# Two programs merged into one at the front of a two-layer kernel: projection 1 and attention A

## The chip, the cores and the metric

The kernel runs on one core of a Trainium2 chip. Its engines have queues of their own: TensorE (PE: matmuls and transposes), VectorE (DVE), ScalarE (ACT), GpSimd (POOL) and SyncE (SP, which issues the DMAs). They meet only at semaphores and at the barriers that stand between two programs. The metric is the device time of one execution in microseconds (us).

## The reference

Two layers over 1024 tokens of width 1024, all in float32. Layer 1:

```
h = rmsnorm(x) * gain
q_a, k_a, v_a, g_a, q_b, k_b, v_b, g_b = split(h @ w_in)      # 512,128,128,512,512,512,512,512 columns
q_a, k_a = rope(rmsnorm(q_a)), rope(rmsnorm(k_a))              # head size 64
o_a = softmax(q_a k_a^T / 8) v_a * silu(g_a)                   # A: 8 query heads, 2 key heads, all 1024 keys
o_b = softmax(q_b k_b^T / 8 + bias, in an 8x16 window) v_b * silu(g_b)   # B: 8 heads
x1 = x + concat(o_a, o_b) @ w_out
```

Layer 2 (a gated delta rule, a dilated attention and a second output projection) follows and is not touched.

## The kernel before

Every float32 matmul operand is split into a rounded high part and a low part (`_hi`, `_lo`), and a product is a sum of passes over these parts. A stage is a program: a `Block` with one function for each engine, entered and left by a barrier of all engines; the `Kit` that owns its semaphores then clears them (`retire`, L66 to L69) behind another barrier. Before B there are two such programs.

**Projection 1** (`stage_project_1`, L449) norms and transposes x, then multiplies it by w_in in 13 chunks of 256 columns. TensorE works through the chunks in order: 0 to 2 give A's queries, keys and values, 3 and 4 A's gates, 5 and 6 B's queries (`qbT`), 7 and 8 B's keys (`kbT`), 9 and 10 B's values, 11 and 12 B's gates. Gates and B's values go by ScalarE to a staging tile of three slots and by DMA to DRAM (`spill`); B's queries and keys are emptied by VectorE (`empty`, L389 and L391). Eight jobs, or four for B's queries and keys, make a chunk; six PSUM banks take them in turn. The weights of a chunk are loaded by SP (`load`, L281), cast to `w_hi` by ScalarE (L312) and subtracted to `w_lo` by GpSimd (L328). SP's order is written out: the load of chunk c+1, then the stores of chunk c. So behind a chunk that is spilled the next load but one waits until that chunk's last store is issued. During chunks 2 to 6 VectorE norms and rotates A's queries and keys. At the end, after chunk 12, GpSimd writes the keys twice side by side (`k_twice`, L529), TensorE transposes them (L543), four blocks at a time, and VectorE writes them as `kk` (L617, L619).

**Attention A** (`stage_attention_a`, L626) has 64 units (a tile of 128 queries, one head) in 16 groups of four. Per group: GpSimd doubles the queries (`q_twice`, L683), TensorE turns them (`turn_q`, L699), ScalarE casts them (L844) and VectorE subtracts (`q_low`, L788). Per unit: scores on TensorE (L712, L713), `row_max` on VectorE (L794), the exponential on ScalarE (L851), eight transposes on TensorE (`turn_probs`, L723), the cast on ScalarE (`probs_high`, L859) and the subtraction on VectorE (`probs_low`, L799). Products with the values (`values`, L737 to L741), their turn back (L750) and the scaled output (`store`, L812, L816) follow two groups behind. VectorE splits A's values (`split_v`, L781, L783) right behind the first `row_max`.

**Attention B** (`neighbourhood_part`, L882) is the first part of the program that follows, `stage_second`. At its start VectorE zeroes two tiles (L1045, L1047), ScalarE casts the first pair's keys (L1088) and VectorE subtracts (L1042), GpSimd places four units' queries on a diagonal (L946, L948), and only then TensorE's first scores can go (L961 to L963). SP loads B's values (L926) there.

Of the kernel before, what the change touches and what calls it, by code (L numbers as in the profile page):

```python
# [18 lines left out]
F32 = mybir.dt.float32  # L19
F32R = mybir.dt.float32r  # L20
ACT = mybir.ActivationFunctionType
ALU = mybir.AluOpType
# [426 lines left out]
def stage_project_1(nc, g, hT_hi, hT_lo):  # L449

    with ExitStack() as ctx:
        k = Kit(nc, ctx)
        ps = k.psum("p1_ps")
        qkv = g.qkv_a

        def kb_dst(base):
            return lambda j: base[:, j // 2, (j % 2) * 512:(j % 2) * 512 + 512]

        chunks = [Chunk(QA0 + c * CW, CW, "act", dst=lambda t, c=c: qkv[:, t, c * CW:(c + 1) * CW]) for c in range(3)]
        chunks += [Chunk(GA0 + c * CW, CW, "act", spill=g.gate1, at=c * CW, silu=True) for c in range(2)]  # L460
        for c in range(2):
            chunks.append(Chunk(QB0 + c * CW, CW, "dve", chan=True, scale=HD ** -0.5, dst=kb_dst(g.qbT[:, 2 * c:2 * c + 2])))
        for c in range(2):
            chunks.append(Chunk(KB0 + c * CW, CW, "dve", chan=True, dst=kb_dst(g.kbT[:, 2 * c:2 * c + 2])))
        chunks += [Chunk(VB0 + c * CW, CW, "act", spill=g.vb, at=c * CW) for c in range(2)]
        chunks += [Chunk(GB0 + c * CW, CW, "act", spill=g.gate1, at=512 + c * CW, silu=True) for c in range(2)]

        ring_x = [g.kbT[:, i, :] for i in range(4)]
        norm = Norm(nc, k, "n1_", g.x, g.gain1, g.ident, hT_hi, hT_lo, ps, ring_x, [g.qbT[:, i, :] for i in range(2)],
                    g.qbT[:, 2, :])  # L470
        pr = Projection(nc, k, "p1_", g.w_in, chunks, hT_hi, hT_lo, ps, norm)
        na_mask = k.sb("na_mask", [P, GRID_W])
        na_loaded = k.sem("na_loaded")
        NH = A_HEADS + A_KV
        tab = k.sb("rope_tab", [P, 2, NT, HD])
        gains = k.sb("rope_gain", [P, 2, 2, HD])
        rot = k.sb("rope_rot", [P, 2, 2, HD])
        tmps = k.sb("rope_tmp", [P, 2 * NH * HD])
        tmp, tmp2 = tmps[:, 0:NH * HD], tmps[:, NH * HD:2 * NH * HD]
        k_twice = tmps[:, 0:2 * 4 * 2 * HD].rearrange("p (n j a d) -> p n j a d", n=2, j=4, a=2)  # L480
        stat = k.sb("rope_stat", [P, 3, NT * NH])
        k_doubled = k.sem("k_doubled")
        tab_loaded = k.sem("tab_loaded")
        var_ready = k.sem("rope_var_ready")
        std_ready = k.sem("rope_std_ready")
        roped = k.sem("roped")
        dve_step = k.sem("rope_step")
        k_transposed = k.sem("k_transposed")
        kk_ready = k.sem("kk_ready")
        n_a = 3 * NT  # L490
        block = ctx.enter_context(nc.Block())

        @block.sync
        def _(sp):
            norm.load(sp, 0)
            sp.dma_start(g.ident[:, :], g.ident_d).then_inc(g.ident_loaded, 16)
            sp.dma_start(g.ones[:, :], g.second["c_ones"]).then_inc(g.ident_loaded, 16)
            norm.load_gain(sp)
            pr.load_half(sp, 0)
            norm.load(sp, 1)  # L500
            pr.load_half(sp, 1)
            norm.load(sp, 2)
            norm.load(sp, 3)
            pr.load(sp, 1)
            for t in range(4, NT):
                norm.load(sp, t)
            pr.load(sp, 2)
            sp.dma_start(tab[:, :, :, :], g.rope).then_inc(tab_loaded, 16)
            sp.dma_start(gains[:, :, :, :], g.gain_a).then_inc(tab_loaded, 16)


            sp.dma_start(na_mask[:, :], g.na_mask).then_inc(na_loaded, 16)
            W = 4 * RIDX * NA_LINE
            for i in range(2):
                band = bass.AP(tensor=g.na_lines.tensor, offset=i * GRID_W * W + GRID_W - 1,
                               ap=[[W - 1, GRID_W], [NA_LINE, 4 * RIDX], [1, GRID_W]])
                sp.dma_start(g.na_table[i * GRID_W:(i + 1) * GRID_W, :, :], band).then_inc(na_loaded, 16)
            pr.sync(sp)

        @block.gpsimd  # L520
        def _(pool):
            pr.gpsimd(pool)
            pool.wait_ge(roped, NT)
            for n in range(2 * A_KV):
                kv, half = n // 2, n % 2
                if n >= 2:
                    pool.wait_ge(k_transposed, n - 1)
                src = qkv[:, 4 * half:4 * half + 4, 512 + kv * HD:512 + (kv + 1) * HD]
                nc.gpsimd.tensor_copy(k_twice[:, n % 2, :, :, :],  # L529
                                      src.unsqueeze(2).to_broadcast([P, 4, 2, HD])).then_inc(k_doubled, 1)  # L530

        @block.tensor
        def _(pe):
            pe.wait_ge(g.ident_loaded, 32)
            pr.first_tensor(pe)
            for c in range(2, len(chunks)):
                pr.tensor_chunk(pe, c)
            for n in range(2 * A_KV):
                pe.wait_ge(k_doubled, n + 1)
                if n >= 2:  # L540
                    pe.wait_ge(kk_ready, n - 1)
                for j in range(4):
                    last = nc.tensor.transpose(ps[:, 6 + n % 2, j * P:(j + 1) * P],  # L543
                                               k_twice[:, n % 2, j, :, :].rearrange("p a d -> p (a d)"), g.ident[:, :])
                last.then_inc(k_transposed, 1)

        @block.scalar
        def _(act):
            pr.first_scalar(act)
            for c in range(2, len(chunks)):  # L550
                pr.split_hi(act, c + 1)
                pr.empty_chunk(act, "act", c)
                if c == 3:
                    act.wait_ge(var_ready, 1)
                    nc.scalar.activation(stat[:, 1, :], stat[:, 0, :], ACT.Sqrt).then_inc(std_ready, 1)

        @block.vector
        def _(dve):
            steps = 0

            def step(op):

                nonlocal steps
                steps += 1
                op.then_inc(dve_step, 1)
                dve.wait_ge(dve_step, steps)

            pr.first_vector(dve)
            for t in range(NT):
                dve.wait_ge(pr.emptied["act"], 2 * NT + t + 1)  # L570
                x = qkv[:, t, 0:NH * HD]
                step(nc.vector.tensor_tensor(tmp[:, :], x, x, ALU.mult))
                step(nc.vector.tensor_reduce(stat[:, 0, t * NH:(t + 1) * NH],
# [46 lines left out]

def stage_attention_a(nc, g):  # L626
# [2593 lines left out]
```

## Time and profile before

| | us |
|---|---|
| median of three runs | 1566.07 |
| lowest and highest run | 1561.85, 1566.69 |
| the profiled execution's own time | 1566.08 |
| its span (first to last instruction) | 1564.3 |
| TensorE busy | 1495.9 |
| VectorE busy | 818.1 |
| ScalarE busy | 628.4 |
| GpSimd busy | 413.6 |

In the trace projection 1 lasts from the start to about 325 us, attention A from there to 546.8 us, and B begins at 547.6 us. A row of the timeline reads: start, length, engine, line, operation, written tile <- read tiles, shapes, count, and in brackets how long the engine had been idle and who released it. Times are us from the start of the span. Names ending in a number (`a_ps0`) are shown without it.

### The profile page before, as it was taken

What the parts mean: (1) busy time and instruction counts of PE and PEld (TensorE: products, weight loads), DVE (VectorE), ACT (ScalarE), POOL (GpSimd) and SP (SyncE); (2) the same over time, 40 slices, a digit from 0 to 9 for tenths busy, and PEclk for the clock granted to TensorE, in tenths of its full rate; (3) what the DMA queues carried; (4) which work ended last, traced back from release to release, by engine and by line L of the source; (5) the groups of instructions that cost most, each with busy time, mean ns of one, the idle gap of its engine ahead of it and who ended that gap; (6) DMA issues with size and microseconds to landing.
All of it is one profiled execution on the core that took longest, in us unless ns stands there. A gap on an engine that the chain in (4) does not pass through costs nothing.

```text
span 1564.3 us, 30384 instructions
## 1 busy us (share of the span) xinstructions
PE 1495.9 (96%) x12386; PEld 1304.0 (83%) x12386; DVE 818.1 (52%) x1511; ACT 628.4 (40%) x1297; POOL 413.6 (26%) x509
## 2 busy tenths in 40 slices
PE   6999999969999889998999999999997998899998
PEld 6999789958878667776799999888896887788887
DVE  5239510068888667744430705362514775888531
ACT  5322011147777467643332212332334443777300
POOL 0212221110000066623202212221206675334430
PEclk9999999989999999999999999999996999999999
DMA  8213102200000032266402335423120011211332
GB/s 251 52 52 108 54 32 73 75 12 1 1 1 1 1 109 59 66 128 188 149 14 37 57 81 89 67 55 53 28 78 26 22 36 56 95 57 59 121 122 81
DMA packets 84465, 103.50 MB, mean 66 GB/s; under 512 B 25375, under 2 KB 68543, under 8 KB 84328
## 3 DMA queue, kind: packets, MB, share of 16 engines
q1 hardware_dynamic: 84328, 101.56, 24.9%
q8 instruction: 100, 1.64, 0.4%
q14 instruction: 37, 0.30, 0.1%
HBM read 78.40 MB, written 23.12 MB: 65 GB/s over the span
## 4 chain that ended last, share of the span: by engine, by line
PE 52%; DVE 2%; ACT 2%; DMA 2%; issue 1%; POOL 1%; SPq 0%; ACTq 0%; DVEq 0%; POOLq 0%
PE s_ps L362 22%; PE s_ps L1174 9%; PE s_ps L2624 2%; PE s_ps L2610 2%; PE s_ps L2002 2%; PE s_ps L1987 2%; PE s_ps L2599 1%; DMA qT<-s_gate 1%; PE s_ps L2038 1%; PE s_ps L992 1%; PE s_ps L2051 1%; PE s_ps L973 1%; PE s_ps L2587 1%; PE s_ps L2600 1%; PE s_ps L1553 1%
## 5 line engine op out<-in xcount | busy, mean ns | idle before, releaser
L328 POOL TENSOR_TENSOR p_w_lo<-p_w_raw,p_w_hi 128x2048 fp32r<-128x2048 f32 (+1 forms) x27 | 127.1, 4707 | 541.2 <-ACT p_w_hi L312 541.2
L362 PE MATMUL s_ps<-p_w_hi,w_out_hi 128*128 128x256 f32 (+1 forms) x640 | 182.0, 284 | 0.1
L362 PE MATMUL s_ps<-p_w_hi,w_out_lo 128*128 128x256 f32 (+1 forms) x640 | 179.7, 281 | 0.0
L362 PE MATMUL s_ps<-p_w_lo,w_out_hi 128*128 128x256 f32 (+1 forms) x640 | 179.5, 281 | 0.0
L362 PE MATMUL p_ps<-p_w_hi,hT_hi 128*128 128x256 f32 x576 | 163.5, 284 | 3.0 <-DVE p_w_lo L322 3.0
L362 PE MATMUL p_ps<-p_w_lo,hT_hi 128*128 128x256 f32 x576 | 162.7, 282 | 0.0
L362 PE MATMUL p_ps<-p_w_hi,hT_lo 128*128 128x256 f32 x576 | 162.6, 282 | 0.0
L362 PEld LDWEIGHTS s_ps<-p_w_hi,w_out_hi 128*128 128x128 f32 x640 | 120.5, 188 | 1.0 <-issue 0.6
L362 PEld LDWEIGHTS s_ps<-p_w_lo,w_out_hi 128*128 128x128 f32 x640 | 120.8, 189 | 0.0
L362 PEld LDWEIGHTS s_ps<-p_w_hi,w_out_lo 128*128 128x128 f32 x640 | 120.6, 188 | 0.0
L312 ACT CAST p_w_hi<-p_w_raw 128x2048 fp32r<-128x2048 f32 (+1 forms) x28 | 53.5, 1909 | 160.2 <-DMA p_w_raw<-w_in 81.7
L362 PEld LDWEIGHTS p_ps<-p_w_hi,hT_hi 128*128 128x128 f32 x576 | 109.1, 189 | 3.4 <-issue 3.3
L362 PEld LDWEIGHTS p_ps<-p_w_lo,hT_hi 128*128 128x128 f32 x576 | 109.2, 190 | 0.0
L362 PEld LDWEIGHTS p_ps<-p_w_hi,hT_lo 128*128 128x128 f32 x576 | 109.0, 189 | 0.0
L799 DVE TENSOR_TENSOR a_pt_lo<-a_ps,a_pt_hi 128x512 fp32r<-128x512 f32 x128 | 82.3, 685 | 24.1 <-ACT a_pt_hi L859 24.1
L859 ACT CAST a_pt_hi<-a_ps 128x512 fp32r<-128x512 f32 x128 | 69.0, 590 | 55.1 <-PE a_ps L723 55.0
L794 DVE TENSOR_REDUCE a_stat<-a_ps 128x1 f32<-128x1024 f32 x64 | 77.8, 1215 | 2.2 <-PE a_ps L713 2.2
L362 PE MATMUL s_ps<-w_out_hi,p_w_hi 128*128 128x512 f32 x192 | 76.2, 397 | 0.0
L362 PE MATMUL s_ps<-w_out_hi,p_w_lo 128*128 128x512 f32 x192 | 75.7, 394 | 0.0
L362 PE MATMUL s_ps<-w_out_lo,p_w_hi 128*128 128x512 f32 x192 | 75.5, 393 | 0.0
L723 PEld LDWEIGHTS a_ps<-ident,tok 128*128 128x128 f32 x512 | 57.7, 142 | 21.3 <-ACT tok L851 17.3
L723 PE MATMUL a_ps<-ident,tok 128*128 128x128 f32 x512 | 69.0, 278 | 6.3 <-ACT tok L851 5.0
(299 smaller groups left out, 3658.3 us busy)
## 6 DMA issues: line engine op xcount, KB each, us to landing
p_w_raw<-w_in SPq DMA_DIRECT2D x27, 1024.0 KB, 8.5
s_gate<-p_spill SPq DMA_DIRECT2D x48, 128.0 KB, 1.8
kbT<-x SPq DMA_DIRECT2D x8, 512.0 KB, 6.4
b_w_raw<-w_out SPq DMA_DIRECT2D x8, 512.0 KB, 5.2
qT<-s_gate SPq DMA_DIRECT2D x8, 512.0 KB, 6.1
qT<-x SPq DMA_DIRECT2D x8, 512.0 KB, 3.2
s_x<-qT SPq DMA_DIRECT2D x8, 512.0 KB, 4.5
c_table<-s_line SPq DMA_DIRECT2D x8, 512.0 KB, 3.7
```

The source lines that it names most:

```text
L312: self.nc.scalar.copy(self.w_hi[:, c % 2, :, 0:w], self.raw[:, :, 0:w]).then_inc(self.w_hi_ready, 1)
L328: ops.tensor_tensor(self.w_lo[:, c % 2, :, 0:w], self.raw[:, :, 0:w], self.w_hi[:, c % 2, :, 0:w].bitcast(F32), ALU.subtract).then_inc(sel ...
L362: last = self.nc.tensor.matmul(out, lhs, rhs, start=(kt == 0 and i == 0), stop=(kt == KT - 1 and i == 2))
L723: last = nc.tensor.transpose(ps[:, 4 + half, j * P:(j + 1) * P], prob(u)[:, c // 2, (c % 2) * P:(c % 2) * P + P], g.ident[:, :])
L794: nc.vector.tensor_reduce(stat[:, 0, u:u + 1], s, AX.X, ALU.max, negate=True).then_inc(max_ready, 1)
L799: nc.vector.tensor_tensor(part(pt_lo, grp, half, i), ps[:, 4 + half, :].rearrange("p (c q) -> p c q", c=4), part(pt_hi, grp, half, i).bitc ...
L859: nc.scalar.copy(part(pt_hi, grp, half, i), ps[:, 4 + half, :].rearrange("p (c q) -> p c q", c=4)).then_inc(pt_hi_ready, 1)
L1174: last = self.nc.tensor.matmul(self.ps[:, 4 + n % 4, :], a, b[:, kt, cols], start=(kt == 0 and i == 0), stop=(kt == KT - 1 and i == 2))
L1987: last = nc.tensor.matmul(own(3)[r, h, :], Al[r, t % 2, l, h, :], X[r, t % 2, h, :], start=True, stop=True)
L2002: last = nc.tensor.matmul(own(4)[r, h, :], T[r, t % 2, h, :], Z[r, h, :], start=True, stop=True)
L2610: last = nc.tensor.transpose(ps[:, 4 + n % 2, (j - first) * P:(j - first + 1) * P], prob[:, u % 3, j * P:(j + 1) * P], g.ident[:, :])
L2624: last = nc.tensor.matmul(ps[q * HD:(q + 1) * HD, 6 + u % 2, 0:HD], prob_t[:, u % 3, j * P + q * HD:j * P + (q + 1) * HD], v[:, j, h * HD: ...
```

## The change

1. Projection 1 and attention A become parts of one program (`stage_first`), with one `Block` and one PSUM tensor. The barriers and the clearing between them are gone. A's tiles lie on memory of projection 1 and on memory to the right that B's early tiles take later, so there are new waits: VectorE waits for all stores of the spill before the first `row_max`, ScalarE for the last job of the projection before the first `probs_high`, and TensorE's first two scores for the emptying of the banks they write.
2. The chunks come in another order: A's gates (3, 4), B's gates (5, 6), B's values (7, 8), B's queries (9, 10), B's keys (11, 12).
3. The keys of A are turned between the first four jobs of chunk 8, and A's first group of queries behind chunk 10; ScalarE and VectorE split that group before the last chunk's jobs are emptied.
4. `split_v` moves from the start of A behind `probs_low` of units 1 and 2.
5. `NearFront`: B's zeroing and the placing of its first four units' queries go to GpSimd, which may start once the values of group 13 are done; the first keys' cast follows ScalarE's last cast of A, the subtraction stands in VectorE's order behind the store of group 14; SP loads B's values once group 14's values are done. B's tiles for these lie to the right, beside `kbT`.
6. The builder is called with a DMA scratch of 2048.

```
-        chunks += [Chunk(GA0 ...spill=g.gate1...) for c in range(2)]      # 3, 4
-        ... QB0 (5, 6), KB0 (7, 8), VB0 (9, 10), GB0 (11, 12)
+    chunks += [Chunk(GA0 ...) ...]      # 3, 4
+    chunks += [Chunk(GB0 ...) ...]      # 5, 6
+    chunks += [Chunk(VB0 ...) ...]      # 7, 8
+    ... QB0 (9, 10), KB0 (11, 12)
+    KEYS_AT, QUERIES_AT = 8, 10
...
+        for c in range(2, len(chunks)):
+            for j in range(chunks[c].jobs):
+                pr.multiply(pe, c, j)
+                if c == KEYS_AT and j < 2 * A_KV:
+                    turn_keys(pe, j)
+            if c == QUERIES_AT:
+                pe.wait_ge(kk_ready, 2 * A_KV)
+                q_turns.turn(pe, 0)
...
+        for i in range(pr.RING):                       # VectorE, before row_max(0)
+            dve.wait_ge(pr.stored[i], 16 * len(range(i, len(pr.spills()), pr.RING)))
...
+            if 1 <= u <= A_KV:
+                split_v(u - 1)
+            if u == n_units + 2:
+                front.vector(dve)
...
+    def gpsimd(pool):
+        for grp in range(2, n_groups):
+            q_turns.double(pool, grp)
+        pool.wait_ge(values_done, n_groups - 2)
+        front.gpsimd(pool)
...
+        sp.wait_ge(values_done, n_groups - 1)
+        front.sync(sp)
...
+class NearFront:
+    def gpsimd(self, pool):
+        self.nc.gpsimd.memset(self.q_diag[:, :, :, :].bitcast(F32), 0.0).then_inc(self.zeroed, 1)
+        self.nc.gpsimd.memset(self.prob[:, :, :], 0.0)
+        pool.wait_ge(self.zeroed, 1)
+        for u in range(self.SLOTS):
+            self.place(pool, u, self.placed, 4 * u)
...
-        nc.vector.memset(prob[:, :, :], 0.0).then_inc(q_zeroed, 1)
-        nc.vector.tensor_copy(q_diag..., prob...)
-        keys_low(0)
```

TensorE where projection 1 ends and attention A begins, before (`rope_tmp` holds the doubled keys, `a_ps` is A's PSUM tensor):

```order
L362 MATMUL p_ps<-p_w_lo,hT_hi 128x256
L362 MATMUL p_ps<-p_w_hi,hT_lo 128x256
L543 MATMUL p_ps<-ident,rope_tmp 128x128 x16
L451 UNCONDITIONAL_BRANCH
L691 UNCONDITIONAL_BRANCH
L699 MATMUL a_ps<-ident,a_q_twice 128x128 x4
L712 MATMUL a_ps<-kk,a_q_hi 128x512
L713 MATMUL a_ps<-kk,a_q_lo 128x512
```

The same place now (one PSUM tensor, `f_ps`):

```order
L362 MATMUL f_ps<-hT_lo,p_w_hi 128x512
L362 MATMUL f_ps<-hT_hi,p_w_lo 128x512
L744 MATMUL f_ps<-kk,a_q_hi 128x512
L745 MATMUL f_ps<-kk,a_q_lo 128x512
L744 MATMUL f_ps<-kk,a_q_hi 128x512
L745 MATMUL f_ps<-kk,a_q_lo 128x512
L744 MATMUL f_ps<-kk,a_q_hi 128x512
L745 MATMUL f_ps<-kk,a_q_lo 128x512
```

The sixteen transposes of keys and the first four of queries have gone to earlier places between projection jobs, and the two branches (the way out of one program and into the next) are gone; scores follow the projection's last matmul.

VectorE at the start of attention A, before:

```order
L619 TENSOR_TENSOR kk<-p_ps,kk 64x512
L451 UNCONDITIONAL_BRANCH
L776 UNCONDITIONAL_BRANCH
L788 TENSOR_TENSOR a_q_lo<-a_ps,a_q_hi 128x512
L794 TENSOR_REDUCE a_stat<-a_ps 128x1
L781 CAST a_v<-tok 128x8x64
L783 TENSOR_TENSOR a_v<-tok,a_v 128x8x64
L781 CAST a_v<-tok 128x8x64
L783 TENSOR_TENSOR a_v<-tok,a_v 128x8x64
L794 TENSOR_REDUCE a_stat<-a_ps 128x1
```

And now:

```order
L391 COPY kbT<-f_ps 128x512 x4
L819 TENSOR_REDUCE a_stat<-f_ps 128x1 x2
L488 TENSOR_TENSOR a_q_lo<-f_ps,a_q_hi 128x512
L824 TENSOR_TENSOR a_pt_lo<-f_ps,a_pt_hi 128x4x128 x2
L819 TENSOR_REDUCE a_stat<-f_ps 128x1
L824 TENSOR_TENSOR a_pt_lo<-f_ps,a_pt_hi 128x4x128 x2
L811 CAST a_v<-tok 128x8x64
L813 TENSOR_TENSOR a_v<-tok,a_v 128x8x64
L819 TENSOR_REDUCE a_stat<-f_ps 128x1
L824 TENSOR_TENSOR a_pt_lo<-f_ps,a_pt_hi 128x4x128 x2
L811 CAST a_v<-tok 128x8x64
L813 TENSOR_TENSOR a_v<-tok,a_v 128x8x64
```

The two halves of `split_v` moved from behind the first row maximum to behind the subtractions of units 1 and 2, and the last copies of B's keys stand directly ahead of the first maxima.

GpSimd at the start of attention B, before (`L68 ISA` clears semaphores):

```order
L683 COPY a_q_twice<-tok 128x512 x16
L634 UNCONDITIONAL_BRANCH
L68 ISA
L3006 UNCONDITIONAL_BRANCH
L946 CAST b_q_diag<-qbT 64x64
L948 TENSOR_TENSOR b_q_diag<-qbT,b_q_diag 64x64
```

And now, with the first of 16 pairs of a cast and a subtraction that stand ahead of the branch:

```order
L468 COPY a_q_twice<-tok 128x512 x14
L994 MEMSET b_q_diag 128x1024
L995 MEMSET b_prob 128x1280
L977 CAST b_q_diag<-qbT 64x64
L979 TENSOR_TENSOR b_q_diag<-qbT,b_q_diag 64x64
```

Zeroing and the first placements moved to the end of A's program; eight such pairs (two for each of four units) follow the memsets before GpSimd reaches the branch.

## Rows read from the trace of the kernel before

**Rows 1.** Waits of TensorE, 0 to 560 us: total, times, longest one.
```profile
PE s_ps L961 <- POOL b_q_diag L948: 5.9, 1, 5.9
...
PE a_ps L699 <- POOL a_q_twice L683: 3.7, 1, 3.7
...
PE p_ps L362 <- DVE qbT L389: 0.3, 1, 0.3
```

**Rows 2.** Timeline, between projection 1 and attention A.
```profile
318.41 1.03 PE L543 MATMUL p_ps<-ident,rope_tmp 128*128 128x128 f32 x8
...
332.62 0.69 DVE L783 TENSOR_TENSOR a_v<-tok,a_v 128x512 fp32r<-128x512 f32 x1
333.22 0.42 DVE L781 CAST a_v<-tok 128x512 fp32r<-128x512 f32 x1
...
333.54 1.77 PE L723 MATMUL a_ps<-ident,tok 128*128 128x128 f32 x8
```

**Rows 3.** Timeline, unit 3 of attention A and the start of unit 4.
```profile
341.85 1.13 ACT L851 ACTIVATE tok<-a_ps,a_stat 128x1024 f32<-128x1024 f32 x1
342.71 1.22 DVE L794 TENSOR_REDUCE a_stat<-a_ps 128x1 f32<-128x1024 f32 x1
...
343.12 1.09 PE L723 MATMUL a_ps<-ident,tok 128*128 128x128 f32 x8 [0.91 <-ACT tok L851]
343.81 1.08 ACT L859 CAST a_pt_hi<-a_ps 128x512 fp32r<-128x512 f32 x2 [0.75 <-PE a_ps L723]
343.97 0.48 PE L712 MATMUL a_ps<-kk,a_q_hi 128*128 128x512 f32 x1
344.43 1.29 DVE L799 TENSOR_TENSOR a_pt_lo<-a_ps,a_pt_hi 128x512 fp32r<-128x512 f32 x2 [0.50 <-ACT a_pt_hi L859]
344.51 0.40 PE L712 MATMUL a_ps<-kk,a_q_hi 128*128 128x512 f32 x1
344.77 1.13 ACT L851 ACTIVATE tok<-a_ps,a_stat 128x1024 f32<-128x1024 f32 x1
```

**Rows 4.** Timeline, the end of attention A and the start of B.
```profile
523.86 0.40 PE L738 MATMUL a_ps<-a_pt_hi,a_v 128*128 128x512 f32 x1
...
544.38 0.69 DVE L806 COPY a_out_t<-a_ps 128x512 f32<-128x512 f32 x1 [5.68 <-PE a_ps L738]
...
546.34 0.42 DVE L816 TENSOR_TENSOR tok<-a_ps,a_stat 128x256 f32<-128x256 f32 x1 [1.18 <-PE a_ps L750]
547.56 0.37 SPq L926 DMA_DIRECT2D b_v<-s_vb  x1
...
549.82 1.16 POOL L946 CAST b_q_diag<-qbT 64x64 fp32r<-64x64 f32 x1 [64.10 <-DVE b_q_diag L1047]
...
552.13 0.80 PE L961 MATMUL s_ps<-b_k_hi,b_q_diag 128*128 128x512 f32 x1 [5.90 <-POOL b_q_diag L948]
```

**Rows 5.** Windows: length; busy PE, PEld, DVE, ACT, POOL; PEclk; DMA share; GB/s.
```profile
345.00:357.00 12.00, 9.72 (x60) 7.55 (x59) 10.20 (x14) 9.21 (x18) 0.62 (x1) 1.00 0.00 1
357.00:400.00 43.00, 42.71 (x256) 34.25 (x255) 37.91 (x55) 31.25 (x58) 2.46 (x4) 1.00 0.00 1
...
537.00:540.00 3.00, 2.26 (x13) 1.79 (x14) 0.52 (x3) 0.00 (x0) 0.00 (x0) 0.96 0.00 0
540.00:543.00 3.00, 3.00 (x9) 2.00 (x8) 0.00 (x0) 0.00 (x0) 0.00 (x0) 0.50 0.00 0
...
552.00:556.00 4.00, 3.50 (x8) 2.14 (x9) 1.40 (x4) 0.87 (x3) 3.14 (x13) 0.50 1.03 394
```

**Rows 6.** Timeline of the projection: GpSimd's weights beside VectorE's rope.
```profile
71.76 4.60 POOL L328 TENSOR_TENSOR p_w_lo<-p_w_raw,p_w_hi 128x2048 fp32r<-128x2048 f32 x1 [7.18 <-ACT p_w_hi L312]
...
72.61 4.43 DVE L572 TENSOR_TENSOR rope_tmp<-tok 128x640 f32<-128x640 f32 x1 [21.73 <-ACT tok L387]
```

**Rows 7.** Timeline of ScalarE, chunk 9's last job and chunk 11's weights.
```profile
250.26 0.39 ACT L387 ACTIVATE p_spill<-p_ps 128x256 f32<-128x256 f32 x1 [2.46 <-PE p_ps L362]
256.57 1.91 ACT L312 CAST p_w_hi<-p_w_raw 128x2048 fp32r<-128x2048 f32 x1 [5.93 <-DMA p_w_raw<-w_in]
```

More of the change, by code:

```diff
@@ L451, in stage_project_1, with stage_first @@
+def stage_first(nc, g, near):
     with ExitStack() as ctx:
         k = Kit(nc, ctx)
[L453 to L480, printed above, removed]
@@ L491, in stage_project_1 @@
+        with ExitStack() as pt_ctx:
+            aside = Kit(nc, pt_ctx, clears=False, side="right")
+            pt_aside = [aside.sb(f"a_pt_{n}", [P, NT, 4 * P], F32R) for n in ("hi1", "lo1", "hi2", "lo2")]
+        front = NearFront(nc, g, near)
+        front.signals(k)
+        attend = attention_a_part(nc, g, k, ps, q_turns, project, pt_aside, front)
         block = ctx.enter_context(nc.Block())
@@ L494, in _ @@
         def _(sp):
[L495 to L517, printed above, removed]
@@ L518, in _ @@
-            pr.sync(sp)
+            project.sync(sp)
+            attend.sync(sp)
         @block.gpsimd
         def _(pool):
[L522 to L530, printed above, removed]
+            project.gpsimd(pool)
@@ L532, in _ @@
+            attend.gpsimd(pool)
         @block.tensor
         def _(pe):
[L534 to L545, printed above, removed]
+            project.tensor(pe)
@@ L547, in _ @@
+            attend.tensor(pe)
         @block.scalar
         def _(act):
[L549 to L555, printed above, removed]
+            project.scalar(act)
+            attend.scalar(act)
         @block.vector
@@ L558, in _ @@
         def _(dve):
[L559 to L573, printed above, removed]
-                                             tmp[:, :].rearrange("p (h d) -> p h d", d=HD), AX.X, ALU.add))
@@ L936, in gpsimd @@
     def gpsimd(pool):
[L937 to L949 removed]
+        for u in range(front.SLOTS, n_units):
+            pool.wait_ge(scores_ready, u - front.SLOTS + 1)
+            front.place(pool, u, q_placed, 4 * (u - front.SLOTS))
     def tensor(pe, op):
@@ L2951, in stage_second @@
             early = Kit(nc, early_ctx, clears=False)
-            near, send = neighbourhood_part(nc, g, early, ps, w_hi, w_lo)
+            near, send = neighbourhood_part(nc, g, early, ps, w_hi, w_lo, front)
             k.owned += early.owned
@@ L3131, in build @@
         g.kbT = first.sb("kbT", [P, 4, SEQ])
-        with ExitStack() as keys_ctx:
-            keys = Kit(nc, keys_ctx, side="right")
-            g.kk = keys.sb("kk", [P, A_KV, SEQ], F32R)
-            with ExitStack() as inner:
-                i = Kit(nc, inner)
-                hT_hi = i.sb("hT_hi", [P, KT, SEQ], F32R)
-                hT_lo = i.sb("hT_lo", [P, KT, SEQ], F32R)
-                stage_project_1(nc, g, hT_hi, hT_lo)
-            stage_attention_a(nc, g)
+        g.kk = first.sb("kk", [P, A_KV, SEQ], F32R)
+        front = stage_first(nc, g, first)
         g.gates = Gates(nc, g, whole)
```

733 lines of the change are left out of this document (429 added, 304 removed).

## The prediction

> **What bounds the kernel now.** I began with the page's busy shares: TensorE has 1495.9 us of a span of 1564.3 us, so at most some 68 us of the time are its gaps, and a change that removes no matmul can only win from those. Then came the waits of TensorE over the first 560 us, where this change lies. The reader should see how few they are [rows 1]: the longest is that of B's first scores for GpSimd's diagonal queries (5.9 us), another that of A's first queries (3.7), and one for a PSUM bank is 0.3. The chain of waits has nothing to say on this stretch, so the timeline had to. It gives two borders. From the slot at 318.41, where the first transpose of A's keys follows the projection's last matmul, to the first transposes of probabilities at 333.54 are 15.1 us [rows 2], in which TensorE does 20 small transposes and two units' scores. From VectorE's last store of A (ends 546.76) to B's first scores at 552.13 are 5.4 us, in which it does nothing [rows 4]. Last the windows: from 357 to 400 us TensorE is busy for 42.71 of 43 us, but from 345 to 357 us, before A's products with values begin, only 9.72 of 12 [rows 5]. So A's first eight units are bound by a loop of ScalarE and TensorE, the rest by TensorE itself, and what the start gains or loses is neither lost nor given back later.
>
> **Border 1, projection to A.** Let 0 be the slot behind the projection's last matmul, the 318.41 of before.
> - Moved in front of it: 20 transposes. Eight took 1.03 us there [rows 2], so 20 are 2.6; eight of probabilities take 0.85 from first start to the next instruction [rows 3], so 20 are 2.1. I take 2.4. They wait for nobody: GpSimd's doubling of the keys stands behind chunk 8's own weights, without which chunk 8 can't start, and rope is over by then, since the bank wait below, behind it in VectorE's order, came in chunk 6. SP's queue is not touched by this move.
> - The bank wait of 0.3 goes [rows 1]: it came from B's queries being due while VectorE was at rope and the bias table, and they come four chunks later now.
> - Scores of unit 0: two matmuls are 0.54 apart [rows 3], four 1.1, and the last one's end makes it 1.2. Their banks were emptied two jobs earlier, the keys and queries long ago. Row maximum 1.22, some 0.05 for the signal, and from the start of an exponential to the transposes 1.27 (341.85 to 343.12) [rows 3]: transposes at 3.8. The wait of VectorE for the stored spill costs nothing, since the last of these stores belongs to chunk 8, some 90 us before.
> - From there 1.65 to the next exponential (343.12 to 344.77), and then 2.92 for each unit [rows 3]: exponentials 1 to 4 at 5.4, 8.3, 11.3, 14.2.
> - `split_v` behind units 1 and 2: 0.42 + 0.69 = 1.11 each [rows 2]. VectorE idles 0.50 per unit [rows 3], and its row maximum is over at 343.93, 0.84 ahead of the exponential that needs it. Followed through: row maximum 3 ends at 11.6 instead of 11.3 at the latest, so +0.4; row maximum 4 at 15.2 against a need of 14.6, so +0.7 more. Together 1.1 (0 if the slack holds it all, 2.2 if none). Exponential 4 stands at 15.3.
> - Before, exponential 4 started at 344.77, that is 26.4 after 318.41. Now 2.4 - 0.3 + 15.3 = 17.4. Gain 9.0.
> - Clock: TensorE now idles 1.3 us ahead of the first transposes and about 0.9 in each unit. In the early units of before a like share of idleness kept 1.00, but at the end of A gaps of that size brought 0.50 (the 1.2 GHz level) for about 3 us [rows 5]. Half speed there would make transposes and their first half later by some 0.4 per unit, one to four units: 0 to 1.6; I take 0.4. Gain 8.6, between 6 and 10.4.
>
> **Border 2, A to B.** The barrier stays. SP issues its first DMA at 547.56, 0.8 us behind VectorE's last store [rows 4]. TensorE's first scores of B now wait for nothing else: 547.7 instead of 552.13, a gain of 4.4. What leaves the border has to be covered:
> - GpSimd: two memsets (2304 elements per partition) and 16 casts and subtractions. Not shown is a large memset on GpSimd; by the rate of its own subtraction of 2048 elements (4.60 us) [rows 6] they are 5.2 us at most, by its shortest rows next to nothing. The placing of unit 0 ran from 549.82 to 552.13, a slow first cast included [rows 4]; four times that is 9.2. So at most 14.4, and I take 8. It may start when group 13's values are done, 524.2 by the times of before [rows 4], which leaves 22.5 until 546.76. Queued behind these on GpSimd is only the barrier.
> - ScalarE's cast has no work of A behind it, VectorE's subtraction falls in the 5.68 us for which it waits on the last group's values [rows 4]. Both cost nothing; without this cover the subtraction, of twice as many elements as the one of 0.69 [rows 2], would cost some 1.4.
> - B's values are loaded by SP once group 14's values are done, ahead of the barrier, so B's weights no longer queue behind them. I give this nothing, since no wait of TensorE names them.
> - Clock: before, B's first 4 us ran at 0.50 behind the idle stretch [rows 5]. Now the gap is 1.6 us, right behind another of 1.2. If it stays fast, three scores at half speed become three at full speed and the first transposes are shorter: up to 1.2 more. I take 0.3. Gain 4.7, between 4 and 5.7.
>
> **Other edits.** The new order holds the same matmuls; six loads are now issued behind a spilled chunk's stores instead of four. Such a load's cast starts 5.93 us after that chunk is emptied [rows 7], and with 1.91 for the cast and 4.60 for GpSimd the weights are ready after 12.4 of the 22.8 us that a chunk of eight jobs at 2.85 lasts [rows 7]: 10.4 us of cover. Zero. The DMA scratch and the place of tiles have no row; I give them zero, with nothing in the profile for either sign.
>
> **Sum.** 8.6 + 4.7 = 13.3; of the profiled execution's own 1566.08 (its span 1564.3 and 1.8 around it, 0.01 from the median of the runs) that leaves 1552.8. From the two borders' bounds: gains of 10 to 16, 1550 to 1556.
>
> **Rivals.**
> 1. Both starts run at full clock: border 1 gives 0.4 more, border 2 0.9 more: 1551.5. For it: both idle gaps are much shorter than the ones of before. Against it: the 0.50 at 540 to 543 us came after gaps of about 1 us [rows 5]. The Trainium skill, "TensorE: Matmul & The Clock Gate", section "HAM oscillation — how this bites in real kernels", warns only of long idle gaps; by that rule this rival would be the likely one, and the trace's row at 540 disagrees.
> 2. GpSimd is late, and B's first scores wait for it as before: border 2 gives nothing, 1557.5. It decides once its work takes over 22.5 us, against my 14.4 at most.
> 3. GpSimd and VectorE shut each other out in A's last units. At 72.61 a VectorE product with both inputs in SBUF took 4.43 us, ending with GpSimd's 4.60 [rows 6]. If that met A's VectorE work too, up to 14.4 us would be added, less the 12% that VectorE idles: some 11.7, and 1564.5. Against it: A's large VectorE operations read PSUM, and B's keys come after GpSimd is done. The Trainium skill, "SBUF — State Buffer", section "SBUF: two separate sides", says that a VectorE operation with two SBUF inputs and a GpSimd one that reads SBUF hold a shared pair of ports for the whole instruction and block each other; by that rule only such pairs meet, and here nearly none does. The 4.43 agrees with the blocking.
> 4. Slower than before: the weights bind. If a load's cast started over 16.3 us after the chunk ahead, instead of 5.93, each of the six chunks would stall; at 18.5 the gain is gone, and at 22 it is 34 us lost, about 1587, or 21 slower than before. The point is far off the row [rows 7], and SP's queue holds nothing new between.
> 5. The change doesn't do what it says: a new wait at border 1 (for stores, for the last job, for banks) holds A back. Half of border 1 gone is 1557; nothing in the order of the queues speaks for it.
>
> **How the numbers follow.** Forecast 0.70, rival 1 0.11, rivals 2 and 5 0.09 together, rival 3 0.04, rival 4 0.03, and 0.03 for what I don't see. What a measurement of this kernel can tell from no change is about 0.3%, 4.7 us: faster is below 1561.4. The forecast, rivals 1, 2 and 5 lie there: 0.89 with a part of the unseen. Rival 3 lies within: 0.07 with a part of it; slower 0.04. The likeliest case's own range is 1550 to 1556; the three runs of before lie 4.8 us apart, and rivals 2 and 5 lie above, so the range is 1548.5 to 1560.
>
> **What would show it.** TensorE's waits for A's first queries and for GpSimd's diagonal gone; the first transposes of probabilities about 4 us behind the projection's last matmul; the projection's end near 320.5; exponential 4 near 336; the fourth and fifth exponentials further apart than 2.92; B's first scores within 1 us of its program's first DMA; GpSimd done with the placements near 533 by the old times. Wrong it would be if chunks 5 to 10 showed waits for weights, if VectorE's subtractions in A's last units were longer than 0.69 each, if the granted clock stayed at 0.50 for long stretches of A, or if the parts behind B, whose order is unchanged, took longer than before.

## The result: 1548.3 us, 18 less than before

| | before | changed |
|---|---|---|
| median of the runs compared, us | 1566.26 (4 runs, 1561.85 to 1566.69) | 1548.30 (4 runs, 1546.77 to 1550.49) |
| span of the profiled execution, us | 1564.3 | 1548.0 |
| mean granted clock of TensorE in it | 0.982 | 0.990 |

The ratio is 0.990 (0.9899), which is 15.8 us, with a 95% interval of 0.9885 to 0.9914: 13.5 to 18.0 us. The two medians are 18 apart. With all later runs of the two kernels the medians are 1566.0 (41 runs) and 1548.2 (11 runs), 17.8 us apart, by resampling 14.5 to 19.4. The forecast was 1552.8 with 1548.5 to 1560: the median lies 0.2 us below the lower end of that range, and the ratio, which puts the changed kernel at 1550.4, inside it.

TensorE's waits of the changed kernel up to 560 us (total, times, longest):

```profile
...
PE f_ps L755 <- ACT tok L872: 6.8, 7, 1.1
PE f_ps L362 <- DVE p_w_lo L322: 3.0, 1, 3.0
PE s_ps L1076 <- PEq L69: 1.6, 1, 1.6
...
```

The three waits of [rows 1] are gone: for A's first queries, for the bank, and for the diagonal, whose 5.9 us have become 1.6 for TensorE's own sequencer behind the barrier. The 3.0 for the first weights stood in before too, and no other wait for weights has come; each of the rows left out has its like in the trace of before. The 6.8 is A's loop of its first units.

The border between projection and attention A, timeline of the changed kernel (beside [rows 2, 3]):

```profile
320.97 0.39 PE L744 MATMUL f_ps<-kk,a_q_hi 128*128 128x512 f32 x1
...
324.72 1.09 PE L755 MATMUL f_ps<-ident,tok 128*128 128x128 f32 x8 [1.11 <-ACT tok L872]
...
330.67 0.69 DVE L813 TENSOR_TENSOR a_v<-tok,a_v 128x512 fp32r<-128x512 f32 x1
...
331.28 1.22 DVE L819 TENSOR_REDUCE a_stat<-f_ps 128x1 f32<-128x1024 f32 x1
...
335.92 1.11 ACT L872 ACTIVATE tok<-f_ps,a_stat 128x1024 f32<-128x1024 f32 x1 [0.36 <-DVE a_stat L819]
```

320.97 is the slot behind the projection's last matmul, the zero of the prediction. The first transposes of probabilities come 3.75 us behind it (15.13 before), exponential 4 (335.92) after 14.95 (26.36 before).

The end of A and the start of B (beside [rows 4]), GpSimd first:

```profile
518.23 0.95 POOL L994 MEMSET b_q_diag<- 128x1024 f32 x1 [41.33 <-PE f_ps L770]
519.12 1.17 POOL L995 MEMSET b_prob<- 128x1280 f32 x1
520.23 0.23 POOL L977 CAST b_q_diag<-qbT 64x64 fp32r<-64x64 f32 x1
...
525.41 0.32 POOL L979 TENSOR_TENSOR b_q_diag<-qbT,b_q_diag 64x64 fp32r<-64x64 f32 x1
```

```profile
529.46 0.43 DVE L841 TENSOR_TENSOR tok<-f_ps,a_stat 128x256 f32<-128x256 f32 x1 [1.18 <-PE f_ps L782]
529.80 1.22 DVE L990 TENSOR_TENSOR b_k_lo<-kbT,b_k_hi 128x1024 fp32r<-128x1024 f32 x1
...
535.97 0.42 DVE L841 TENSOR_TENSOR tok<-f_ps,a_stat 128x256 f32<-128x256 f32 x1 [1.18 <-PE f_ps L782]
537.44 0.82 SPq L1232 DMA_DIRECT2D b_w_raw<-w_out  x2
...
537.48 0.47 PE L1076 MATMUL s_ps<-b_k_hi,b_q_diag 128*128 128x512 f32 x1 [1.62 <-PEq L69]
```

GpSimd is done at 525.73, 10.7 us ahead of A's last store; VectorE's subtraction lies in its wait for the last group. B's first scores start 1.09 us behind that store (5.37 before), 0.04 behind SP's first DMA.

Windows of the changed kernel at the places of [rows 5] (columns as there):

```profile
530.00:534.00 4.00, 3.94 (x16) 2.50 (x16) 1.02 (x1) 0.00 (x0) 0.00 (x0) 1.00 1.00 378
534.00:537.00 3.00, 1.10 (x8) 0.97 (x8) 1.20 (x3) 0.00 (x0) 0.00 (x0) 1.00 0.37 138
537.00:540.00 3.00, 1.62 (x6) 1.05 (x6) 1.39 (x4) 0.81 (x3) 1.23 (x5) 1.00 0.49 132
```

The granted clock is 1.00 in A's last products and at B's start, where before had 0.50 (the 1.2 GHz level) at both. From this trace alone one would write: forecast 13.3, measured 16.3 in the spans (1564.3 and 1548.0), and the 3 us between are the clock, as rival 1 had it. The experiments were made to test that.

### The profile page after: what moved, and what is told of

It is laid out like the page before. It is cut to its first block, busy times and chain, and to the rows that moved or that the text cites. A ratio compares the mean times of both kernels' runs of the same rounds, so it can differ in the third digit from the quotient of the medians.

```text
span 1548.0 us, 30361 instructions
## 1 busy us (share of the span) xinstructions
PE 1485.2 (96%) x12386; PEld 1296.9 (84%) x12386; DVE 812.8 (53%) x1509; ACT 627.1 (41%) x1297; POOL 413.6 (27%) x511
## 4 chain that ended last, share of the span: by engine, by line
PE 52%; DMA 2%; DVE 2%; ACT 2%; issue 1%; POOL 1%; SPq 0%; ACTq 0%; DVEq 0%; POOLq 0%
PE s_ps L362 23%; PE s_ps L1281 9%; PE s_ps L2731 2%; DMA qT<-s_gate 2%; PE s_ps L2717 2%; PE s_ps L2109 1%; PE s_ps L2094 1%; PE s_ps L2706 1%; PE s_ps L2145 1%; PE s_ps L1107 1%; PE s_ps L2158 1%; PE s_ps L1088 1%; PE s_ps L2694 1%; PE s_ps L2707 1%; PE s_ps L1267 1%
## 5 line engine op out<-in xcount | busy, mean ns | idle before, releaser
L362 PE MATMUL f_ps<-p_w_hi,hT_hi 128*128 128x256 f32 x576 | 163.7, 284 | 3.0 <-DVE p_w_lo L322 3.0
L362 PE MATMUL f_ps<-p_w_hi,hT_lo 128*128 128x256 f32 x576 | 162.6, 282 | 0.0
L362 PE MATMUL f_ps<-p_w_lo,hT_hi 128*128 128x256 f32 x576 | 162.6, 282 | 0.0
L362 PEld LDWEIGHTS f_ps<-p_w_hi,hT_hi 128*128 128x128 f32 x576 | 109.0, 189 | 3.3 <-issue 3.3
L362 PEld LDWEIGHTS f_ps<-p_w_lo,hT_hi 128*128 128x128 f32 x576 | 109.0, 189 | 0.0
L362 PEld LDWEIGHTS f_ps<-p_w_hi,hT_lo 128*128 128x128 f32 x576 | 109.0, 189 | 0.0
L824 DVE TENSOR_TENSOR a_pt_lo<-f_ps,a_pt_hi 128x512 fp32r<-128x512 f32 x128 | 82.3, 685 | 23.8 <-ACT a_pt_hi L880 23.8
L880 ACT CAST a_pt_hi<-f_ps 128x512 fp32r<-128x512 f32 x128 | 68.9, 590 | 54.8 <-PE f_ps L755 54.8
L872 ACT ACTIVATE tok<-f_ps,a_stat 128x1024 f32<-128x1024 f32 x64 | 72.4, 1131 | 44.1 <-DVE a_stat L819 44.0
L819 DVE TENSOR_REDUCE a_stat<-f_ps 128x1 f32<-128x1024 f32 x64 | 77.6, 1214 | 0.3 <-PE f_ps L745 0.3
```

What stands on the lines that cost most here:

```text
L362: last = self.nc.tensor.matmul(out, lhs, rhs, start=(kt == 0 and i == 0), stop=(kt == KT - 1 and i == 2))
L819: nc.vector.tensor_reduce(stat[:, 0, u:u + 1], s, AX.X, ALU.max, negate=True).then_inc(max_ready, 1)
L824: nc.vector.tensor_tensor(part(pt_lo, grp, half, i), ps[:, 4 + half, :].rearrange("p (c q) -> p c q", c=4), part(pt_hi, grp, half, i).bitc ...
L872: nc.scalar.activation(prob(u), s, ACT.Exp, bias=stat[:, 0, u:u + 1], accum_out=stat[:, 1, u:u + 1]).then_inc(prob_ready, 1)
L880: nc.scalar.copy(part(pt_hi, grp, half, i), ps[:, 4 + half, :].rearrange("p (c q) -> p c q", c=4)).then_inc(pt_hi_ready, 1)
```

## The experiments

Each kernel's time is given with the median of before on the same chip and, where it was repeated, the ratio with its interval. "Exponential 4" and the zero are the prediction's.

**order_only**: the kernel before, two programs, with the new order of chunks and the keys turned in chunk 8.

```diff
+        chunks += [... GB0 ...]; chunks += [... VB0 ...]      # then QB0, KB0
-            for n in range(2 * A_KV): pe.wait_ge(k_doubled, n + 1) ...
+                    if c == 8 and j < 2 * A_KV:
+                        turn_keys(j)
```

> The kernel before with two edits of the change alone: the new order of chunks, and A's keys turned between the jobs of chunk 8; two programs and both barriers stay. Theory (waits and the clock): the border of the two programs is left as soon as VectorE has copied the last bank, some 3.9 us earlier than before, the keys' 1.6 us of TensorE now lie inside the projection, and A still starts behind an idle stretch at 0.50 of the clock: 1562.5, 3.5 to 4 us less than before. Rival (the order itself is worth more, by the bank wait and the queues): 1559 or less. Rival (the border costs what it costs, whoever comes last): 1566.

1558.8 us (before 1567.4; 0.995, 0.9929 to 0.9967). The zero is at 320.70, exponential 4 at 340.33, so 19.6 instead of 26.4: the order with the turned keys is worth 6.7 of border 1's 11.4 us (less some 1.8 for the sixteen transposes), the single program 4.7. The waits that stay are those of the second program's start:

```profile
323.15 0.66 PE L704 MATMUL a_ps<-ident,a_q_twice 128*128 128x128 f32 x4 [2.31 <-POOL a_q_twice L688]
...
325.21 0.51 PE L717 MATMUL a_ps<-kk,a_q_hi 128*128 128x512 f32 x1 [1.40 <-DVE a_q_lo L793]
```

In the trace of before the same two rows are

```profile
326.39 1.12 PE L699 MATMUL a_ps<-ident,a_q_twice 128*128 128x128 f32 x4 [3.71 <-POOL a_q_twice L683]
...
328.91 0.79 PE L712 MATMUL a_ps<-kk,a_q_hi 128*128 128x512 f32 x1 [1.40 <-DVE a_q_lo L788]
```

The instructions are the same, but from the turn of the queries to the first exponential they take 5.89 us there and 4.70 here, since the clock falls to 0.50 at 324.8 us there, ahead of both rows, and at 326.1 here, 0.9 us behind the start of the scores. So 1.2 of the 6.7 are the clock.

The time fell as far as the rival's (1559 or less) and by more than this border explains. Of the 7.4 us between the spans 2.4 lie behind B's first values (1003.3 us instead of 1005.7), where nothing was changed.

**old_order**: the changed kernel with the old order of chunks, keys still turned in chunk 8.

```diff
+        chunks: QB0 (5, 6), KB0 (7, 8), VB0 (9, 10), GB0 (11, 12)
+        vector: for chunk 8, pr.empty(...) and keys(j) in turn; q_turns.low(dve, 0) last
```

> The changed kernel with the chunks in the order of before (A's gates, B's queries, B's keys, B's values, B's gates); one program, keys turned in chunk 8 (now B's second keys), the first queries behind chunk 10 but split only after ScalarE has emptied the last bank. Theory: scores of unit 0 start 1.9 us later, the bank wait of 0.3 is back, and the wait of VectorE for the last stored spill is covered by the scores or costs up to 1 us: 1550.5 to 1551.5. Rival (the stores take longer): 1553 or more. Rival (the order of the chunks is worth nothing once there is one program): 1548.3.

1552.3 us (before 1567.4; 0.991, 0.9881 to 0.9943). A's first scores wait 1.68 us for the queries' low part, and exponential 4 stands at 16.9 instead of 14.95. So the order is worth 2 us of its own once there is one program; the 4 us between the medians are within the spread.

**front_late**: the changed kernel with border 2 undone, GpSimd, ScalarE, VectorE and SP preparing B at B's start (the zeroing stays with GpSimd).

```diff
-        pool.wait_ge(values_done, n_groups - 2)
-        front.gpsimd(pool)             # and front.scalar, front.vector, front.sync in A
+        front.gpsimd(pool)             # at the start of B
```

> The changed kernel with border 2 undone: B's zeroing, first placements (all on GpSimd), first keys and the load of B's values stand again at the start of B's program. Theory (waits and the clock): B's first scores come 3.6 us later (two memsets 2.1, one unit's placing 1.4), and behind 4.7 us of idleness TensorE starts B at 0.50 again, 1.4 us more: 1553.3. Rival (waits alone): 3.6 us more, 1551.9, with the clock at 1.00. Rival (B's values now land too late): above 1555.

1554.2 us (before 1567.4; 0.992, 0.9898 to 0.9936), 5.9 above the changed kernel's median (2.8 by the two ratios). Timeline at B's start:

```profile
538.92 1.23 DVE L981 TENSOR_TENSOR b_k_lo<-kbT,b_k_hi 128x1024 fp32r<-128x1024 f32 x1 [2.11 <-ACT b_k_hi L978]
...
541.38 0.79 PE L1067 MATMUL s_ps<-b_k_hi,b_q_diag 128*128 128x512 f32 x1 [5.10 <-POOL b_q_diag L970]
```

The scores come 4.58 us behind A's store, 3.5 later than in the changed kernel, and at half speed (0.79 us instead of 0.47). GpSimd is last, VectorE 1.2 us ahead of it.

**pool_early**: GpSimd's part alone stays in A's last units.

```diff
-        front.scalar(act)              # in A, also front.vector(dve) and front.sync(sp)
+        keys_high(0)                   # at the start of B, also keys_low(0) and front.sync(sp)
```

> The changed kernel with only GpSimd's part (two memsets, four placements) left in A's last units; the first keys' cast and subtraction and the load of B's values are back at B's start. Theory: B's first scores wait for VectorE's subtraction, which ended 3.8 us behind A's last store where everything was at B's start, so the border is 3.5 to 3.8 us instead of 1.1 (changed kernel) and 4.6 (all at B's start), with the clock low behind it: 1548.3 plus 2.5 plus 1.0 = 1551.8. Rival (GpSimd's part is the one that counts, as the wait of before names it): border at most 2 us, 1549 to 1550.

1554.3 us (before 1564.1; 0.994, 0.9919 to 0.9959), with

```profile
541.90 0.80 PE L1068 MATMUL s_ps<-b_k_hi,b_q_diag 128*128 128x512 f32 x1 [3.92 <-DVE b_k_lo L982]
...
548.71 0.47 PE L1099 MATMUL s_ps<-b_v,b_prob_t 128*64 128x64 f32 x9 [0.87 <-DMA b_v<-s_vb]
```

The border is 3.40 us: taking away the wait that the trace of before names gives 1.2, the one hidden behind it 2.3 more. The early load of B's values, to which the prediction gave nothing, is worth 0.9 as soon as the scores are early and the load is not. The time is 2.5 us above the expected 1551.8; in the trace 1.5 of them are a low stretch in A's last products.

**v_pool**: the splitting of A's values on GpSimd instead of VectorE.

```diff
-            if 1 <= u <= A_KV: split_v(u - 1)      # VectorE
+        split_v(0); split_v(1)                     # GpSimd, behind the projection's last job
```

> The changed kernel with A's values split on GpSimd in place of VectorE, behind the projection's last job. Theory: exponentials 3 and 4 are no longer delayed, 0.7 us less: 1547.6. Rival (GpSimd's operations with two SBUF inputs shut VectorE out): 1 to 3 us more than the changed kernel, VectorE's subtractions longer than 0.69. Rival (lost in what follows): no change, 1548.3.

1548.9 us (before 1567.4; 0.988, 0.9862 to 0.9905), not to be told from the changed kernel. Exponential 4 stands at 14.23 instead of 14.95: `split_v` costs 0.7 us on VectorE, forecast 1.1. But B's first scores come 1.5 us behind A's last store, here and in pool_and_fill, and 1.1 in the six other traces with a prepared front. So 0.4 of the 0.7 is lost again at border 2; why is open.

**v_first**: `split_v` where before had it.

```diff
         row_max(0)
+        split_v(0)
+        split_v(1)
```

> The changed kernel with both splits of A's values behind the first row maximum, where the kernel before had them, instead of behind units 1 and 2. Theory (the cost is VectorE's, wherever the 2.2 to 2.5 us stand): the second exponential comes 3.7 us behind the first as in the kernel before (3.66 there, 2.97 in the changed kernel), the next ones 2.92 to 3.0 apart, and exponential 4 stands at 15.0 us behind the projection's last matmul, as in the changed kernel (14.95). Rival (spreading them is worth something): 15.4 or more. The time is 1546 to 1550 in both cases.

1549.2 us (before 1567.0, one run each). The exponentials are 3.60, 3.00, 2.91 and 2.93 apart, exponential 4 stands at 14.9. So in this one trace the place of `split_v` is worth nothing, and only its length counts.

**before_again** and **after_again**: second traces of both kernels.

> The kernel before, unchanged, for a second trace of it. Two theories on the low clock (0.50, the 1.2 GHz level) that the first trace showed during the products of A's last group of values (539.6 to 543.2 us). Theory: it is bound to no instruction and falls now here, now there, so this trace has it at another place or not at all; with it gone, exponential 4 to the end of A's last store is 200.4 us instead of 202.0. Rival: the two programs of before cause it, and it stands at the same group again, within 1 us, with 202.0. In both cases B's first scores run at 0.50 behind the 5.4 us gap, and the first products with values come 6.0 to 6.5 us behind them.

> The changed kernel, unchanged, for a second trace of it. Theory (the low clock wanders): 1546.5 to 1550.5 us, and a low stretch may now stand in A's end or at B's start, of up to 1.5 us in cost. Rival (one program keeps it away): 1.00 from 295 to 590 us as in the first trace, exponential 4 to the last store's end 200.4, and B's first products 5.0 us behind its first scores.

1569.5 and 1546.7 us. The windows of before_again, as in [rows 5]:

```profile
537.00:540.00 3.00, 1.69 (x11) 1.11 (x9) 1.20 (x3) 0.00 (x0) 0.00 (x0) 1.00 0.00 0
540.00:543.00 3.00, 2.85 (x13) 1.99 (x13) 0.00 (x0) 0.00 (x0) 0.00 (x0) 1.00 0.00 0
...
552.00:556.00 4.00, 3.62 (x10) 2.25 (x11) 1.40 (x4) 1.15 (x3) 3.16 (x12) 0.50 1.02 386
```

The 0.50 at 540 us, on which the prediction's doubt about rival 1 rested, is not there the second time, in the same program; from exponential 4 to the end of A's last store it is 200.43 us instead of 201.99. The low stretch at B's start came back. after_again stayed at 1.00 from 295 to 590 us.

**before_fill**: the kernel before with transposes of the identity in TensorE's idle time.

```diff
+                if u >= n_units: fill(6 if u % 4 in (1, 2) else 0)     # end of A
+        for _ in range(38):                                            # start of B
+            nc.tensor.transpose(ps[:, 1, 0:P], g.ident[:, :], g.ident[:, :])
```

> The kernel before with transposes of the identity, whose result nobody reads, in TensorE's idle time: six ahead of each turn back and of each group's first product after A's last unit, and 38 (about 4.1 us) ahead of B's first scores, while these wait for GpSimd. No wait is taken away. Theory (the clock falls behind idle time and its price at B's start is 1.4 us, at A's end 1.5): B's first scores start where they did, at full clock (first matmul 0.48 instead of 0.79 us), the first products with values 5.0 us behind them, and the time is 1563.4 to 1565 (2.9 or 1.4 less than before). Rival (the clock at these places costs nothing in the end, other waits take its place): 1566.3, no change. If the fill itself runs at half clock it ends late, and the time is up to 4 us longer.

1565.7 us (before 1564.1; 1.001, 0.9999 to 1.0029). In the trace the fill does what it should:

```profile
547.72 4.34 PE L1004 MATMUL s_ps<-ident 128*128 128x128 f32 x38 [1.37 <-PEq L69]
...
552.24 0.50 PE L967 MATMUL s_ps<-b_k_hi,b_q_diag 128*128 128x512 f32 x1 [0.18 <-POOL b_q_diag L954]
```

The scores start no earlier, run at 1.00 and the first values follow after 5.27 us instead of 6.44 and 6.60. But the median didn't fall. The interval reaches from 0.2 us less to 4.5 us more, so the 1.4 to 2.9 us less that were expected, and the 1.2 us by which B's first values are nearer, lie outside it. The clock behaves in the trace as the theory has it, and the time speaks for the rival: what was won at B's start doesn't arrive at the end. What takes its place is open.

**after_third**: the changed kernel once more, beside more runs of before.

> The changed kernel, unchanged, with five rounds beside the kernel before. By the stretches of two traces of each (projection's end +1.9, from there to exponential 4 -11.4, store to B's first scores -4.3, from these to the first values -1.5) the change is worth 15.3 us: ratio 0.990, 1549 us where before has 1564. Rival: the 18 us of the first four runs are the true gain, ratio 0.9885. Exponential 4 at 14.95 behind the projection's last matmul, border between A and B 1.1 us, both as in the first two traces.

1548.5 us (6 runs, 1542.9 to 1555.1; before 1566.3; 0.990, 0.9871 to 0.9920). Exponential 4 at 14.94, the border 1.09. The interval holds both the 15.3 us that were expected from the traces' stretches and the 18 of the first runs, so it doesn't decide between them. The clock at B's start now fell (first values after 5.75 us). In v_first it fell ahead of the first scores, which is this row:

```profile
536.92 0.77 PE L1076 MATMUL s_ps<-b_k_hi,b_q_diag 128*128 128x512 f32 x1 [1.62 <-PEq L69]
```

**fill_delta** and **pool_and_fill**: 49 such transposes in the idle time at the delta rule's start (layer 2, far behind the change), the second with v_pool's edit.

```diff
+                if t == 0: fill(3)       # ahead of khat_turn; fill(10) ahead of gram
+                if t == 0 and l == 1: fill(36)
```

> The changed kernel with 49 transposes of the identity, whose result nobody reads, in TensorE's idle time at the start of the delta rule's stage (3, 10 and 36 of them, ahead of its gaps of 0.8, 1.5 and 4.7 us), far behind the change. Theory (low stretches of the clock, which follow idle time, are what is left of the run-to-run spread and cost some us each): the granted clock stays 1.00 from 1160 to 1190 us, where every trace so far shows 13 to 20 us at 0.50, and the stretch from the first update of the inverse to the causal attention's first scores (142.5 to 146.4 us so far) takes 139 to 141: the whole kernel 1545 us, 2 to 4 less. Rival (that stretch is bound by VectorE and ScalarE): the clock is full and the time the same within 1 us. If the fill falls into half clock itself, it ends 4 us late and the kernel is 2 to 4 us slower.

> The fill of the delta rule's start together with A's splitting of values on GpSimd instead of VectorE. Theory: both gains add, 0.7 at A's start (exponential 4 at 14.2 us behind the projection's last matmul instead of 14.95) and 2 to 4 at the delta rule: 1544.5 us, the fastest of all. Rival: neither shows beyond the spread of runs, 1547 to 1548.5.

1544.9 us (before 1566.3; 0.986, 0.9841 to 0.9883) and 1544.2 us (0.987, 0.9848 to 0.9887). The ten runs of the two have a mean of 1545.2, the eleven of the changed kernel 1548.9; shuffled, such a difference comes up in 1.3% of the cases. Windows of TensorE alone (length, busy PE, PEclk, DMA share, GB/s) of the changed kernel:

```profile
1160.00:1170.00 10.00, 4.40 (x52) 0.71 0.05 15
1170.00:1180.00 10.00, 7.69 (x84) 0.50 0.16 42
1180.00:1190.00 10.00, 7.89 (x149) 0.77 0.01 2
```

of fill_delta:

```profile
1160.00:1170.00 10.00, 9.35 (x103) 1.00 0.05 15
1170.00:1180.00 10.00, 7.41 (x95) 0.69 0.14 42
1180.00:1190.00 10.00, 8.33 (x134) 0.63 0.01 2
```

and of pool_and_fill:

```profile
1160.00:1170.00 10.00, 9.35 (x103) 1.00 0.07 22
1170.00:1180.00 10.00, 7.18 (x144) 1.00 0.14 42
1180.00:1190.00 10.00, 8.46 (x153) 1.00 0.18 43
```

In fill_delta the fill kept the clock up while it ran and the clock fell behind it; in pool_and_fill it stayed up, and this stretch (first update of the inverse to the causal attention's first scores) took 139.0 us, against 142.2 to 146.4 in the thirteen other traces. In fill_delta it took 143.7, so the 139 to 141 expected of it didn't come, though its median did: one trace shows the theory and one doesn't. Both medians are below every other version's and not to be told from each other; that v_pool's 0.7 adds to the fill is not shown.

## Why the prediction was right, and where its sizes were off

The stretches of all traces of the two kernels, in us:

| stretch | before | changed | gain | forecast |
|---|---|---|---|---|
| first transposes to the zero | 310.5, 311.7 | 311.4, 311.7, 312.6 | -0.8 | -2.1 |
| zero to exponential 4 | 26.4, 26.3 | 14.95, 14.95, 14.94 | 11.4 | 11.1, less 0.4 for the clock |
| to the end of A's last store | 202.0, 200.4 | 200.5, 200.5, 200.3 | 0.8 | 0 |
| to B's first scores | 5.4, 5.4 | 1.1, 1.1, 1.1 | 4.3 | 4.4 |
| to B's first values | 6.4, 6.6 | 5.0, 5.0, 5.8 | 1.3 | 0.3 |
| to the end | 1005.7, 1009.3 | 1005.5, 1003.8, 1002.8 | 3.5 | 0 |

**Border 1** stands. Scores, row maximum and exponential gave the 3.8 that were forecast (3.75), `split_v` 0.7 instead of 1.1. The two exponentials behind it came 0.26 and 0.47 late, where 0.4 and 0.7 had been followed through. Half speed among A's first units, for which 0.4 was put in, came in none of ten traces of a single program, while all four of two programs had it (0.74 to 0.83 between 320 and 330 us). The moved transposes cost what was forecast: four stand in 0.36 us between two matmuls, and the next matmul takes 0.08 more, so 20 are 2.2 against 2.4. The -0.8 of the table is not at odds with this, since this stretch alone varies by 1.2 between runs of one kernel.

**Border 2** stands in its waits. GpSimd took 7.5 us against the 8 taken. One row was misread: group 13's values were not done at 524.2 but one unit later, near 527.0 by the old times (its last two key tiles follow at the next group's start). That left 19.8 us instead of 22.5, and decided nothing. Rivals 2 and 3 fall with it: GpSimd was 10.7 us early, and VectorE's subtractions in A's last units took 0.685 us each, as before. The Trainium skill, "SBUF — State Buffer", section "SBUF: two separate sides", is not at odds with this: beside GpSimd's work VectorE's operations read PSUM, but for a reciprocal with one input, so no pair of a two-input VectorE operation and a reading GpSimd one met there. Such a pair did meet at A's start in before, and there the trace agrees with it:

```profile
333.68 1.09 DVE L783 TENSOR_TENSOR a_v<-tok,a_v 128x512 fp32r<-128x512 f32 x1
```

This is `split_v`'s second subtraction, begun 0.07 us behind a copy of 0.62 us on GpSimd. In all five traces where the two overlapped, VectorE's took 1.04 to 1.09 us, and 0.69 in each of the other 19 rows. The section also counts VectorE operations in a two-port mode among those that meet GpSimd, which the prediction left out. Rival 4 falls too, as no wait for weights came; rival 5 likewise.

**The clock** is where the sizes were off, and where the first trace misled. Read alone, it gives rival 1 right: full speed at both starts, and 1.5 us more in A's last products. Over all fourteen traces it reads otherwise. The low stretch in A's last products is in five (two of four with two programs, three of ten with one) and costs 1.5 us each time. At B's start the eight traces with a prepared front took 5.0, 5.0, 5.75, 5.8, 6.9, 7.0, 7.0 and 7.0 us to the first values, a mean of 6.2, and the three with two programs and no fill 6.0, 6.4 and 6.6. So the change doesn't bring the full clock at B's start; it only leaves it open. The forecast's 0.3 was nearer to the mean than the 1.4 of the first pair of traces. The prediction's step that failed is its reading of the 0.50 at 540 us as a result of gaps of about 1 us: the same gaps in the same program gave 1.00 in the next execution. The Trainium skill, "TensorE: Matmul & The Clock Gate", section "HAM oscillation — how this bites in real kernels", warns of long idle gaps. At the delta rule's start nine of the twelve traces without a fill there agree with it: the clock fell within a gap of 5.5 us. In before, before_again and the first trace of the changed kernel it fell 1.6 to 2.5 us ahead of the gap (4.7 to 4.8 us in these), within or just behind one of 1.5 us; these, like the stretches at the end of A behind gaps of 0.7 to 1.2 us, are not covered by that section.

**What the sum leaves.** The two borders by their waits give 11.4 + 4.3 less 2.2 for the transposes plus 0.3 for the bank: 13.8, against 13.3 forecast. All runs together say 17.8 (14.5 to 19.4); the first four alone (13.5 to 18.0) don't exclude 13.8. The forecast put everything outside the borders at nothing, so that the measured time stands at the lower end of its range and not outside it is owed to the range's width there, and to no term of the sum. Of the 4.0 us between, about 2 are seen behind B's first values, and the rest isn't located. Behind B's first values the four traces with two programs took 1003.3 to 1009.3 us (mean 1005.9), the eight with one program and no fill 1001.7 to 1005.5 (mean 1003.8). All four of the former show a low clock between 1310 and 1350 us, of the latter four of eight.

The table's 3.5 us in this part, from the traces of the two kernels alone, stand in a single stretch, that from the first update of the inverse to the causal attention's first scores: 146.4 us in both traces of before, 143.9, 142.5 and 142.2 in the changed kernel. Around its start before ran at the low clock for 27.3 us in both traces, the changed kernel for 20.5, 13.7 and 13.7. Windows of TensorE in before:

```profile
1170.00:1180.00 10.00, 7.38 (x79) 0.90 0.13 42
1180.00:1190.00 10.00, 4.56 (x56) 0.50 0.12 37
1190.00:1200.00 10.00, 9.06 (x120) 0.50 0.02 5
1200.00:1205.00 5.00, 4.43 (x57) 0.50 0.02 5
```

But order_only and before_fill, with two programs as well, had 13.7 us of it and took 142.7. So two programs don't force it. Whether a single program makes low stretches rarer, or these executions happened to fall this way, stays open: it was not tried, and the spread within either group is as large as the difference.

In the prediction's chances, those of the forecast, rival 1 and rivals 2 and 5 add up to 0.90, and not to the 0.89 given for all of them with a part of the unseen.

## What to carry to other kernels

A border between two programs costs more than its barrier: also the first chain of small dependent steps behind it, which ran at half speed in part in all four traces with two programs. Take that chain apart by the timeline, and move each piece in front of the border under the wait of an engine that idles; when the named wait is gone, the next one may be an engine that was done only 1 us ahead of it, as here (front_late, pool_early). A forecast from waits was good to half a microsecond, one from the granted clock of a single trace was not: take two or three traces of the kernel before, and charge to the change only what differs in all of them.

## What the runs showed of the hardware

- The granted clock is not fixed by the program. Low stretches come and go between executions of one kernel, and with them the time: over 35 runs of before, a line through time and mean granted clock falls by 0.9 us for each 0.001 (correlation -0.77), from 1569.95 at 0.981 to 1560.57 at 0.988.
- Idle time filled with transposes keeps the clock up while the fill runs (1.00 from 1160 to 1170 us instead of 0.71), but it may fall behind it.
- GpSimd's memset of 128x1024 took 0.95 us, of 128x1280 1.17; by the subtraction's rate [rows 6] they would have been 2.3 and 2.9 (an estimate).
- GpSimd's first small cast in B's program took 1.16 us [rows 4] in all four traces where it stood first, and the later ones 0.23. With two memsets ahead of it in the same program (front_late) it took 0.29.
- A VectorE subtraction with both inputs in SBUF took 1.04 to 1.09 us instead of 0.69 when it began beside a GpSimd copy (five traces of five).
